# The order of a TensorE queue in one kernel: values of an attention unit ahead of the logits over cached keys

## Chip, cores, metric

One core of a Trainium2 chip (trn2) runs the whole program in one launch. The metric is the device time of an execution in microseconds. Times below are of single executions, their median, or of the one execution that the hardware profiler recorded.

## What is computed

One inference step of a two-layer decoder trunk, for a prompt group (1 x 1024 tokens) and a sample group (8 sequences x 8 new tokens, each with 1024 cached keys and values in pages). Layer 0 has stick-breaking attention beside a linear recurrence, layer 1 a chunked mixing layer; each is followed by a convolutional FFN. The part in question is the attention of layer 0, for the prompt (8 heads of 64, blocks of 128 queries) and for the samples over their caches:

```python
def sb_attend(q, k, v, bias, q_pos, k_pos):
    z = einsum('bqhd,bkhd->bhqk', q, k) * (HD_A ** -0.5) + bias
    causal = k_pos[None, :] < q_pos[:, None]
    log_keep = where(causal, log_sigmoid(-z), 0.0)
    log_after = cumsum(log_keep, axis=3, reverse=True) - log_keep
    w = where(causal, exp(log_sigmoid(z) + log_after), 0.0)
    return einsum('bhqk,bkhd->bqhd', w, v)

def sb_cached(q, k, v, bias, k_past, v_past):   # the samples: past = 1024 keys in pages, 8 new ones
    return sb_attend(q, concat([k_past, k]), concat([v_past, v]), bias, past + arange(8), arange(past + 8))
```

The kernel works with products of the probabilities 1 - sigmoid(z) instead of sums of logarithms: a scan multiplies them from the right, and the result times sigmoid(z) is the weight.

## The kernel before

**Phases.** `phase_even` does the attention, the recurrence and the projections of layer 0; a barrier of all engines follows; then `phase_rest` does the output projection of layer 0 and everything after it. The change lies in `phase_even` alone.

**Units.** `attention_units` cuts the prompt's attention into 48 units: 4 pairs of heads, for each 8 blocks of 128 queries, with at most 512 keys a unit, so that the last four blocks are two units each. A unit has n = 128 to 512 keys. For unit u:

- *logits* (TensorE, line 950, and 957 for the mask) writes two banks of PSUM, one per head;
- ScalarE takes two sigmoids from each (line 1172, `keep` and `take`);
- VectorE scans `keep` (line 1384); GpSimd multiplies `take` by it (1350, 1352);
- *weights* (TensorE, line 969) transposes n/128 tiles a head, into two banks "T";
- the copies out of these into `weights_transposed` follow: head 0 on ScalarE (line 1180), head 1 on VectorE (line 1393, `transposed`);
- *values* (TensorE, line 988, function `values`) multiplies them with `v_tokens_pair0` or `v_tokens_pair1`: 2 x n/128 matmuls, one query block's sum, which VectorE copies out (line 1403).

**Slots.** The order of work is written out by hand. `slot_order` gives the keys of a slot, and every engine walks through the same list and picks out its own. A slot has the logits of unit u and the transposes of unit u - 1; the values of unit u - 1 come behind all keys of the slot. Steps -1 to 2 lay projections between these. Step 3 has 13 slots, 0 to 12, where u runs from 36 to 48 (slot 12 has no logits, and the values of the last unit, 47). There the attention over the cached keys lies between the units, from `cached_items`. A third of it, three slots, belongs to one pair of samples s = 2p, 2p + 1:

- slots 1, 4, 7, 10 ("first slots"): L L K K K K | T T | K K K K, then W W W of the pair before (not in slot 1), then Z of the even sample;
- slots 2, 5, 8, 11: L L, V of the pair before (in slot 2: N), K K K | T T | K;
- slots 3, 6, 9, 12 ("third slots"): L L K K K K | T T | Z of the odd sample, F of the pair before (in slot 12 F stands ahead of Z; in slot 3 there is none), then the sigmoids of the pair.

Here L are a unit's logits and T its transposes. K (line 1008) transposes a cached key page's 128 columns for 512 keys, into a bank that ScalarE (line 1212) or VectorE (line 1517) empties into `ktr`, the buffer of transposed keys, of which there is one. Z (line 1022, `cached_logits`) is 8 matmuls of 512 columns over `ktr`, which add up in banks 3 and 4. W (1046, 1050) transposes the cached weights, V (1065, 1069; `last_values`, 1083 and 1087, for the last pair) multiplies them with the cached values, F (1097) gathers a pair's output. After Z of the odd sample the pair's sigmoids run on ScalarE (lines 1237 and 1239; for the last pair 1231 and 1233 in halves), then VectorE scans and multiplies (1522 and 1526; 1537 and 1542). N and P are small and run once each.

In the program's names `x_residual` holds, in this phase, `keep`, `ktr` and other buffers, `take_then_weights` holds `take`, `squares_then_scale` the samples' queries, and `v_tokens_pair` or `xb_padded` the pair's sigmoids.

**Waits.** Each engine does its queue in order. `values(u)` waits until both copies of T of unit u are done, and, where the unit opens a new sum, until the sum before it has been copied out. `cached_logits(s)` waits until the last two K of the sample (parts 6 and 7) have been copied. Semaphore `qk_done` tells the end of Z, `pv_done` that of values.

Of the kernel before, what the change touches and what calls it, by code (L numbers as in the profile page):

```python
# [547 lines left out]
def slots_of(step):  # L548
    return range(len(SIDE) + (step == 3))


def slot_order(step, slot, units):

    per = len(units) // 4
    u = per * step + slot
    first = [("L", u, 0), ("L", u, 1)] if 0 <= u < len(units) else []
    turned = [("T", u - 1, 0), ("T", u - 1, 1)] if u > 0 else []
    opened = [("O", u - 1, 0)] if u > 0 and units[u - 1][5] else []
    items = [(kind, which, group) for s, kind, which, group in side_items(step) if s == slot]
    if step < 3 or slot == 0:  # L560
        return first + turned + items + opened
    items = cached_items(slot)
    return first + items[0:4] + turned + items[4:] + opened
# [61 lines left out]
def phase_even(core, mix, k_sample, spill):  # L625
# [6 lines left out]
    with ExitStack() as ctx:  # L632
# [96 lines left out]
        def wait_emptied(eng, key):  # L729
            for who, count in banks.emptied[key]:  # L730
                eng.wait_ge(emptied_by[who], count)
# [144 lines left out]
        def in_order(step, slot):  # L876
            return slot_order(step, slot, units)

        @block.tensor
        def _(pe):  # L880
            def free(key):
                if banks.before[key]:
                    wait_emptied(pe, banks.before[key])

            def project(key, middle=None):
                kind, c, group = key
                n = slab_number(kind, group)
                a, b = CUT_USED[c]
                free(key)
                if c == 0:  # L890
                    w.wait_ready(pe, n)
                mm = None
                for k in range(KT):
                    if k == 6 and middle:
                        middle()
                    col = slice(k * P, (k + 1) * P)
                    for s, (wt, xt) in enumerate(((w.hi, act_hi), (w.lo, act_hi), (w.hi, act_lo))):
                        mm = pe.matmul(bank(key, 0, b - a), wt[:, n % 2, col], xt[:, k, a:b], start=k == 0 and s == 0,
                                       stop=k == KT - 1 and s == 2)
                mm.then_inc(filled, 1)  # L900
# [41 lines left out]
            def logits(u):  # L942
                pair, qb, lo, n, diagonal, _, _ = units[u]
                if u % PER == 0:
                    pe.wait_ge(normed, 2 * pair + 2)
                for h in range(2):
                    b = h * HD
                    key = ("L", u, h)
                    free(key)
                    mm = pe.matmul(bank(key, 0, n), mix[b:b + HD, pair, qb * P:(qb + 1) * P],  # L950
                                   kt[pair % 2][b:b + HD, lo:lo + n], start=True, stop=not diagonal,
                                   skip_group_check=True)
                    if not diagonal:
                        mm.then_inc(filled, 1)
                if diagonal:
                    for h in range(2):
                        pe.matmul(bank(("L", u, h), n - P, n), core.ident16[:, :], core.unseen[:, :], start=False,
                                  stop=True, skip_group_check=True).then_inc(filled, 1)

            def weights(u):  # L960
                n = units[u][3]
                for h in range(2):
                    key = ("T", u, h)
                    free(key)
                    pe.wait_ge(weighted, 2 * u + h + 1)
                    if not units[u][4]:
                        pe.wait_ge(edged, banks.edges[u] - 1 + h)
                    for q in range(n // P):
                        mm = pe.transpose(bank(key, q * P, (q + 1) * P), take[u % 2][h][:, q * P:(q + 1) * P],
                                          core.ident[:, :])  # L970
                    mm.then_inc(filled, 1)
# [3 lines left out]
            def values(u):  # L975
                pair, qb, lo, n, _, opens, closes = units[u]
                if u % PER == 0:
                    wait_emptied(pe, ("vt", 2, pair))
                if opens:
                    opened[pair, qb] = ("O", u, 0)  # L980
                    free(("O", u, 0))
                o = banks.bank[opened[pair, qb]]
                wait_emptied(pe, ("T", u, 0))
                wait_emptied(pe, ("T", u, 1))
                for q in range(n // P):
                    for h in range(2):
                        b = h * HD
                        mm = pe.matmul(core.ps[b:b + HD, o, 0:P], vtok[pair % 2][:, lo // P + q, b:b + HD],
                                       wtr[:, h, q * P:(q + 1) * P], start=opens and q == 0,
                                       stop=closes and q == n // P - 1, skip_group_check=True)  # L990
                mm.then_inc(pv_done, 1)

            def states():
                free(("P", 0, 0))
                pe.wait_ge(h_ready, 4)
                for j in range(4):
                    mm = pe.transpose(bank(("P", 0, 0), j * P, (j + 1) * P, 36), pk[:, j, :], core.ident[:, :])
                mm.then_inc(pk_tr, 1)
# [12 lines left out]
            def cached_logits(s):  # L1011
                u, a = s // 2, s % 2
                wait_emptied(pe, ("K", s, 6))
                wait_emptied(pe, ("K", s, 7))
                pe.wait_ge(qd_ready, 5)
                for h in range(2) if s < NSEQ - 1 else (1, 0):
                    if a == 0:
                        free(("Z", u, h))
                    if s == NSEQ - 1 and h == 0:
                        mm.then_inc(z_last, 1)  # L1020
                    for c in range(4):
                        mm = pe.matmul(core.ps[32 * c:32 * c + 32, 3 + h, :], qd[:, c, s, :],
                                       ktr[:, c, h * 512:(h + 1) * 512], start=a == 0, stop=a == 1,
                                       skip_group_check=True)
                mm.then_inc(qk_done, 1)
# [77 lines left out]
            for step in range(-1, 4):  # L1103
                for slot in slots_of(step):
                    u = PER * step + slot
                    pending = u > 0 and step < 3
                    for key in in_order(step, slot):
                        kind, which, part = key
                        if kind == "L" and part == 0:
                            logits(which)  # L1110
                        elif kind == "T" and part == 0 and step == 3:
                            weights(which)
                        elif kind in SLABS:
                            if (kind, part) == ("x", 0):
                                continue
                            project(key, (lambda: weights(u - 1)) if pending else None)
                            pending = False
                            if key == ("q", 1, 0):
                                norm.sums_pe(pe)
                        elif kind in ("r", "i"):  # L1120
                            gate(key)
                        elif kind in ("qs", "ks"):
                            square_sums(key)
                        elif kind in ("vt", "kt"):
                            rows(key)
                        elif kind == "P":
                            states()
                        elif kind == "N":
                            new_logits()
                        elif kind == "K":  # L1130
                            cached_keys(which, part)
                        elif kind == "Z":
                            cached_logits(which)
                        elif kind == "W":
                            cached_weights(which, part)
                        elif kind == "V":
                            cached_values(which)
                        elif kind == "F":
                            cached_finish(which)
                    if u > 0:  # L1140
                        values(u - 1)
            for part in (2, 1, 0):
                cached_weights(3, part)
# [1800 lines left out]
```

## Time and profile before

| | us |
|---|---|
| median of 3 runs | 2646.26 |
| the 3 runs | 2646.66, 2644.01, 2646.26 |
| the profiled execution, its own time | 2647.26 |
| its span in the trace | 2645.5 |

| engine | busy us | share of the span |
|---|---|---|
| TensorE, matmul (PE) | 2593.1 | 98% |
| VectorE (DVE) | 1608.0 | 61% |
| GpSimd (POOL) | 1132.3 | 43% |
| ScalarE (ACT) | 867.7 | 33% |

Times in rows count from the start of the span. An idle time in brackets stands ahead of a row, with what ended it. Step 3 runs from about 412 to 544 us, and is followed by the barrier. A row of matmuls counts each fp32 matmul twice: it is done in two passes.

### The profile page before, as it was taken

Reading aid. Unit: us, or ns where it says so; the run is one execution under the profiler, and the core shown is the slowest. Engines: PE = TensorE matmul, PEld = TensorE weight load, DVE = VectorE, ACT = ScalarE, POOL = GpSimd, SP = SyncE. Lnnn points to the kernel's source line nnn. Section 1 sums busy time; section 2 is a strip of 40 time slices with the busy share of each in tenths; the row PEclk is TensorE's granted clock in tenths of the full one; section 3 lists DMA queues with packets and bytes.
Section 4 is the critical chain, followed back from the end, with each engine's and each line's share of the span. In section 5 each row is a group of like instructions: output and inputs, shape, how many; then the busy total and the mean of one; then the engine's idle time right before and its main releaser. Section 6 shows DMA issues by size and latency. Waiting matters only on the chain.

```text
span 2645.5 us, 42776 instructions
## 1 busy us (share of the span) xinstructions
PE 2593.1 (98%) x16013; PEld 2423.5 (92%) x16013; DVE 1608.0 (61%) x2183; ACT 867.7 (33%) x1229; POOL 1132.3 (43%) x919
## 2 busy tenths in 40 slices
PE   8999998899999999999999999999999999999999
PEld 7878885689999999999999999999999999999998
DVE  6456566632666666666766544524766677766674
ACT  5575665533222222222222534423222222222221
POOL 3234333224544544445554411344554555544541
PEclk9999999999999999999999999999999999999999
DMA  5101107831111111111111211211111111111112
GB/s 178 57 25 44 43 25 236 274 133 41 56 49 48 48 48 48 41 47 48 48 48 33 57 40 37 60 45 56 56 41 48 48 48 48 48 40 47 48 32 71
DMA packets 208446, 164.11 MB, mean 62 GB/s; under 512 B 9902, under 2 KB 182039, under 8 KB 208335
## 3 DMA queue, kind: packets, MB, share of 16 engines
q1 hardware_dynamic: 207278, 160.35, 19.6%
q8 instruction: 79, 1.29, 0.2%
q10 hardware_dynamic: 576, 2.10, 0.2%
q14 instruction: 33, 0.26, 0.0%
q0 software_dynamic: 480, 0.11, 0.0%
HBM read 147.83 MB, written 14.69 MB: 61 GB/s over the span
## 4 chain that ended last, share of the span: by engine, by line
PE 78%; DVE 0%; ACT 0%; issue 0%; DVEq 0%
PE psum_all L148 50%; PE psum_all L2002 16%; PE psum_all L2476 6%; PE psum_all L2016 2%; PE psum_all L1990 1%; PE psum_all L1992 1%; PE psum_all L2528 0%; PE psum_all L2492 0%; PE psum_all L2516 0%; PE psum_all L2346 0%; PE psum_all L2562 0%; PE psum_all L1670 0%; DVE mixed_odd L2687 0%; ACT operand_hi_a L1775 0%; PE psum_all L2533 0%
## 5 line engine op out<-in xcount | busy, mean ns | idle before, releaser
L108 POOL TENSOR_TENSOR w_lo_part<-w_raw,w_hi_part 128x1024 fp32r<-128x1024 f32 x94 | 227.5, 2421 | 577.7 <-ACT w_hi_part L104 577.7
L2234 DVE TENSOR_TENSOR x_residual<-x_residual,psum_all 128x512 f32<-128x512 f32 (+1 forms) x616 | 449.9, 761 | 19.4
L148 PE MATMUL psum_all<-operand_hi_c,w_hi_part 128*128 128x364 f32 (+1 forms) x1344 | 297.6, 330 | 0.6 <-DVE operand_lo_c L1779 0.6
L148 PE MATMUL psum_all<-operand_hi_a,w_hi_part 128*128 128x364 f32 (+1 forms) x1344 | 297.9, 330 | 0.2 <-DVE operand_lo_a L1779 0.2
L148 PE MATMUL psum_all<-operand_hi_c,w_lo_part 128*128 128x364 f32 (+1 forms) x1344 | 295.6, 328 | 0.0
L148 PE MATMUL psum_all<-operand_lo_a,w_hi_part 128*128 128x364 f32 (+1 forms) x1344 | 295.4, 328 | 0.0
L148 PE MATMUL psum_all<-operand_hi_a,w_lo_part 128*128 128x364 f32 (+1 forms) x1344 | 295.2, 328 | 0.0
L148 PE MATMUL psum_all<-operand_lo_c,w_hi_part 128*128 128x364 f32 (+1 forms) x1344 | 295.0, 328 | 0.0
L113 POOL TENSOR_TENSOR w_lo_part<-w_raw,w_hi_part 128x1024 fp32r<-128x1024 f32 x54 | 130.6, 2419 | 373.6 <-ACT w_hi_part L97 373.6
L2218 DVE TENSOR_TENSOR gate_conv_ffn<-psum_all,gate_conv_ffn 128x1092 f32<-128x1092 f32 x48 | 62.2, 1296 | 347.3 <-PE psum_all L148 347.3
L2002 PE MATMUL psum_all<-hidden_hi_ffn,w_down_hi_ffn 128*128 128x512 f32 x616 | 240.9, 391 | 0.0
L2002 PE MATMUL psum_all<-hidden_hi_ffn,w_down_lo_ffn 128*128 128x512 f32 x616 | 240.7, 391 | 0.0
L2002 PE MATMUL psum_all<-hidden_lo_ffn,w_down_hi_ffn 128*128 128x512 f32 x616 | 239.9, 389 | 0.0
L148 PEld LDWEIGHTS psum_all<-operand_hi_a,w_hi_part 128*128 128x128 f32 x1344 | 233.5, 188 | 4.2 <-DVE operand_lo_a L1779 0.5
L148 PEld LDWEIGHTS psum_all<-operand_hi_c,w_hi_part 128*128 128x128 f32 x1344 | 233.1, 188 | 4.4 <-issue 0.8
L148 PEld LDWEIGHTS psum_all<-operand_hi_c,w_lo_part 128*128 128x128 f32 x1344 | 233.5, 188 | 0.0
L148 PEld LDWEIGHTS psum_all<-operand_hi_a,w_lo_part 128*128 128x128 f32 x1344 | 233.3, 188 | 0.0
L148 PEld LDWEIGHTS psum_all<-operand_lo_a,w_hi_part 128*128 128x128 f32 x1344 | 232.2, 188 | 0.0
L148 PEld LDWEIGHTS psum_all<-operand_lo_c,w_hi_part 128*128 128x128 f32 x1344 | 232.2, 188 | 0.0
L104 ACT ACTIVATE w_hi_part<-w_raw 128x1024 fp32r<-128x1024 f32 x94 | 99.7, 1062 | 401.1 <-PE psum_all L148 401.1
L1914 POOL TENSOR_TENSOR gate_conv_ffn<-gate_conv_ffn,rms_scale 128x1092 f32<-128x1092 f32 x48 | 122.4, 2549 | 187.8 <-ACT gate_conv_ffn L2103 187.8
L1352 POOL TENSOR_TENSOR take_then_weights<-take_then_weights,x_residual 128x511 f32<-128x511 f32 (+3 forms) x96 | 94.8, 998 | 163.6 <-DVE x_residual L1384 124.7
(354 smaller groups left out, 5042.3 us busy)
## 6 DMA issues: line engine op xcount, KB each, us to landing
w_raw<-in_w_gate_dram SPq DMA_DIRECT2D x48, 512.0 KB, 3.8
w_raw<-in_w_up_dram SPq DMA_DIRECT2D x48, 512.0 KB, 3.8
w_down_raw_ffn<-in_w_down_dram SPq DMA_DIRECT2D x44, 512.0 KB, 4.2
k_pages<-in_cache_k_dram SPq DMA_DIRECT2D x64, 256.0 KB, 3.7
v_pages<-in_cache_v_dram SPq DMA_DIRECT2D x64, 256.0 KB, 5.5
w_raw<-in_w_in_even_dram SPq DMA_DIRECT2D x20, 512.0 KB, 4.0
w_raw<-in_w_in_odd_dram SPq DMA_DIRECT2D x16, 512.0 KB, 4.8
x_spill<-x_residual SPq DMA_DIRECT2D x8, 546.0 KB, 5.3
```

Source lines behind the costliest of these rows:

```text
L104: act.activation(dst, self.raw[:, raw, :], ACT.Copy).then_inc(self.s_hi, 1)
L108: pool.tensor_tensor(lo, self.raw[:, raw, :], hi.bitcast(F32), ALU.subtract).then_inc(self.s_lo, 1)
L113: pool.tensor_tensor(dst if dst is not None else self.lo[:, par, :], self.raw[:, par, :], (hi if hi is not None else self.hi[:, par, :]).b ...
L148: mm = pe.matmul(bank[:, c, 0:width(c)], w, x[:, chunk(c)], start=(k == 0 and step == 0), stop=(k == last and step == 2))
L1352: pool.tensor_tensor(t[:, 0:n - 1], t[:, 0:n - 1], k[:, 1:n], ALU.mult).then_inc(weighted, 1)
L1914: pool.tensor_tensor(gc, gc, self.core.rb[:, :], ALU.mult).then_inc(self.gr_ready, 1)
L1990: pe.matmul(rows, b.h_smp[:, k, :], self.blocks(b.d_hi, p, 0)[:, cols], start=start and p % 2 == 0 and k == 0, stop=False, skip_group_chec ...
L2002: mm = pe.matmul(core.ps[:, base + bank, :], wt, xt[:, x, :], start=first and step == 0, stop=step == 2, skip_group_check=True)
L2016: mm = pe.matmul(bank[:, c, 0:width(c)], wt, x[:, chunk(c)], start=(k == 0 and step == 0), stop=(k == 1 and step == 2))
L2218: dve.tensor_tensor(gc, bank[:, :, 0:CH], gc, ALU.mult).then_inc(self.evac, 1)
L2234: dve.tensor_tensor(dst, dst, src, op).then_inc(self.pair_read, 1)
L2476: mm = pe.matmul(self.core.ps[:, self.lane_bank(f), 0:width(c)], wm[:, is_u, col], xm[:, k, chunk(c)], start=k == 0 and s == 0, stop=k == ...
```

## The change

In the slots that have a Z, the values of unit u - 1 are put in front of Z. In all other slots they stay at the end. There are eight Z, in the first slots 1, 4, 7, 10 and the third slots 3, 6, 9, 12. Only the TensorE queue is changed: the lists of ScalarE, VectorE, GpSimd and the DMA queue are what they were.

```diff
                     pending = u > 0 and step < 3
+                    summed = u == 0
                     for key in in_order(step, slot):
...
                         elif kind == "Z":
+                            if not summed:
+                                values(u - 1)
+                                summed = True
                             cached_logits(which)
...
-                    if u > 0:
+                    if not summed and u > 0:
                         values(u - 1)
```

TensorE's queue in slot 1, the first one with a Z: `v_tokens_pair` (L988) are the values, `x_residual,squares_then_scale` (L1022) is Z.

```order
 L1008 MATMUL psum_all<-identity,k_pages 128x128 x16
+L988 MATMUL psum_all<-weights_transposed,v_tokens_pair 64x128 x2
 L1022 MATMUL psum_all<-x_residual,squares_then_scale 32x512 x8
-L988 MATMUL psum_all<-weights_transposed,v_tokens_pair 64x128 x2
 L950 MATMUL psum_all<-x_residual,mixed_even 128x384 x2
```

The two matmuls of the values stand between the last K and Z now. T (L969) lies ahead of those 16 K.

The same engine in slot 3, where T is the last thing ahead of Z:

```order
 L1008 MATMUL psum_all<-identity,k_pages 128x128 x16
 L969 MATMUL psum_all<-identity,take_then_weights 128x128 x6
+L988 MATMUL psum_all<-weights_transposed,v_tokens_pair 64x128 x6
 L1022 MATMUL psum_all<-x_residual,squares_then_scale 32x512 x8
-L988 MATMUL psum_all<-weights_transposed,v_tokens_pair 64x128 x6
 L950 MATMUL psum_all<-x_residual,mixed_even 128x128 x2
```

The values stand right behind the transposes whose copies they read, and Z behind both.

The same engine in slot 12, the last, where the transposes of the cached weights (L1046, L1050) follow:

```order
 L969 MATMUL psum_all<-identity,take_then_weights 128x128 x8
 L1097 MATMUL psum_all<-query_selector,own_outputs 128x32 x2
+L988 MATMUL psum_all<-weights_transposed,v_tokens_pair 64x128 x8
 L1022 MATMUL psum_all<-x_residual,squares_then_scale 32x512 x8
-L988 MATMUL psum_all<-weights_transposed,v_tokens_pair 64x128 x8
 L1046 MATMUL psum_all<-identity,v_tokens_pair 8x128
```

The values stood between Z and W here; now Z and W are neighbours.

## Rows read from the trace of the kernel before

**Rows 1.** Windows: busy time by engine, step 3 and all after it.
```profile
core 0: us, PE busy (x) PEld busy (x) DVE busy (x) ACT busy (x) POOL busy (x), PEclk, DMA share, GB/s
412.00:545.00 133.00, 109.67 (x1372) 77.49 (x1372) 73.39 (x101) 64.65 (x124) 26.32 (x31) 0.95 0.77 258
545.00:2645.50 2100.50, 2092.27 (x12080) 2009.76 (x12080) 1289.93 (x1721) 549.42 (x721) 953.39 (x733) 1.00 0.16 50
```

**Rows 2.** Timeline, slot 1: start us, us, engine, line, operation [idle before <-releaser].
```profile
422.92 0.28 DVE L1393 COPY weights_transposed<-psum_all 128x128 f32<-128x128 f32 x1
...
425.54 0.69 DVE L1517 COPY x_residual<-psum_all 128x512 f32<-128x512 f32 x1 [0.41 <-PE psum_all L1008]
...
426.33 1.92 PE L1022 MATMUL psum_all<-x_residual,squares_then_scale 128*32 128x512 f32 x16 [0.83 <-ACT x_residual L1212]
...
428.19 0.44 PE L988 MATMUL psum_all<-weights_transposed,v_tokens_pair 128*64 128x128 f32 x4
```

**Rows 3.** Timeline, slot 4: Z of the third sample.
```profile
451.60 1.92 PE L1022 MATMUL psum_all<-x_residual,squares_then_scale 128*32 128x512 f32 x16
```

**Rows 4.** Timeline, slots 3 and 4: Z, values, and the way back to TensorE.
```profile
440.19 0.54 DVE L1393 COPY weights_transposed<-psum_all 128x384 f32<-128x384 f32 x1
...
440.37 1.92 PE L1022 MATMUL psum_all<-x_residual,squares_then_scale 128*32 128x512 f32 x16 [1.03 <-ACT weights_transposed L1180]
...
442.22 0.88 PE L988 MATMUL psum_all<-weights_transposed,v_tokens_pair 128*64 128x128 f32 x12
442.35 1.11 ACT L1237 ACTIVATE xb_padded<-psum_all,row_bias 128x1024 f32<-128x1024 f32 x1 [2.44 <-PE psum_all L1022]
...
443.49 2.31 DVE L1522 TENSOR_TENSOR_SCAN xb_padded<-xb_padded,all_ones 128x1032 f32<-128x1032 f32 x1 [2.76 <-ACT xb_padded L1237]
...
448.24 0.66 PE L969 MATMUL psum_all<-identity,take_then_weights 128*128 128x128 f32 x4 [1.53 <-DVE x_residual L1517]
```

**Rows 5.** Timeline, slots 6 and 7.
```profile
466.99 1.93 PE L1022 MATMUL psum_all<-x_residual,squares_then_scale 128*32 128x512 f32 x16
467.07 0.69 DVE L1393 COPY weights_transposed<-psum_all 128x512 f32<-128x512 f32 x1 [0.18 <-PE psum_all L969]
...
469.84 1.09 PE L988 MATMUL psum_all<-weights_transposed,v_tokens_pair 128*64 128x128 f32 x16
...
478.12 1.53 PE L1008 MATMUL psum_all<-identity,k_pages 128*128 128x128 f32 x12 [1.52 <-DVE x_residual L1517]
```

**Rows 6.** Timeline, slots 9 and 10.
```profile
499.00 0.54 DVE L1393 COPY weights_transposed<-psum_all 128x384 f32<-128x384 f32 x1
499.17 1.93 PE L1022 MATMUL psum_all<-x_residual,squares_then_scale 128*32 128x512 f32 x16 [1.24 <-issue]
...
501.59 0.88 PE L988 MATMUL psum_all<-weights_transposed,v_tokens_pair 128*64 128x128 f32 x12
...
509.89 1.53 PE L1008 MATMUL psum_all<-identity,k_pages 128*128 128x128 f32 x12 [1.15 <-DVE x_residual L1517]
```

**Rows 7.** Timeline, slot 12 and what follows it.
```profile
527.93 0.69 DVE L1393 COPY weights_transposed<-psum_all 128x512 f32<-128x512 f32 x1 [0.18 <-PE psum_all L969]
...
528.19 1.92 PE L1022 MATMUL psum_all<-x_residual,squares_then_scale 128*32 128x512 f32 x16
...
530.04 1.09 PE L988 MATMUL psum_all<-weights_transposed,v_tokens_pair 128*64 128x128 f32 x16
...
532.16 0.27 PE L1046 MATMUL psum_all<-identity,v_tokens_pair 128*8 128x128 f32 x1 [1.03 <-DVE v_tokens_pair L1542]
...
534.08 1.09 PE L1050 MATMUL psum_all<-identity,v_tokens_pair 128*128 128x128 f32 x4 [1.17 <-DVE v_tokens_pair L1542]
```

**Rows 8.** Windows around the end of the step; the granted clock is in column PEclk.
```profile
530.00:534.00 4.00, 1.89 (x25) 1.36 (x21) 3.89 (x5) 2.58 (x6) 0.00 (x0) 1.00 0.67 249
534.00:540.80 6.80, 6.72 (x104) 4.97 (x108) 0.14 (x1) 0.58 (x1) 0.00 (x0) 0.50 0.02 5
```

**Rows 9.** Timeline, cached values at the one clock and at the other.
```profile
455.53 1.96 PE L1065 MATMUL psum_all<-v_pages,x_residual 128*32 128x128 f32 x64
...
535.68 1.94 PE L1087 MATMUL psum_all<-v_pages,x_residual 128*32 128x128 f32 x32
```

## Prediction, made before the changed kernel had run

> **What bounds the kernel now.** I read the windows first [rows 1]. Behind the barrier, from 545 us on, TensorE is busy 2092.27 of 2100.50 us; whatever the change shifts in front of the barrier, that part follows by the same amount, since its first work waits for the barrier and nothing in it has room to catch up. So the question is by how much step 3 ends earlier or later. In step 3 TensorE is busy 109.67 of 133.00 us, 23 us idle; VectorE has 73.39 and ScalarE 64.65. No engine is full, so the step is bound by TensorE's queue together with the handovers to and from ScalarE and VectorE. Next I read the timeline slot by slot, at the eight Z: did TensorE wait ahead of Z, for what, when had the copies been done that the values read, and who waits for the end of Z?
>
> **What the change removes, adds and moves.** No instruction is added or removed. Eight groups of values move ahead of Z. Each edit has two effects: values fill a wait ahead of Z, if their own inputs have come by then; and Z ends later by the length of the values plus any wait for their inputs. Successive groups overlap by some 0.07 us (the Z row is 1.92 us long and the next row starts 1.86 later [rows 2]), so the values of slot 1 cost 0.37 us where their row shows 0.44, and by the same step 0.81 and 1.02 where rows show 0.88 and 1.09. An engine's end reaches TensorE some 0.1 us later: in slot 1 VectorE's copy of the last K ends at 425.54 + 0.69 = 426.23, and Z starts at 426.33 [rows 2]. I take 0.09.
>
> *First slots (1, 4, 7, 10).* The four K behind T give the copies of T time to end. In slot 1 the copy was done at 423.20, and TensorE stood idle 0.83 us ahead of Z, for the copies of the last K [rows 2]. The values, 0.37 us, fit into that. Z starts as before, and the next logits start 0.37 us earlier: **-0.37 us**. In slot 4, W lies between the K and Z, and Z starts with no wait [rows 3]; slots 7 and 10 read the same. There Z is exchanged with values at no gap: the next logits start when they did, and Z's later end (1.02 us in slot 4) is waited for by nobody soon, because these are even samples, whose sum goes on with the odd sample two slots later; the next copies into `ktr` come only behind V and a unit's logits. **0 us** for three slots. If that cover were gone, each would cost the length of its values, up to 1.02.
>
> *Third slots (3, 6, 9, 12).* Here T is the last thing ahead of Z. The change puts the values right behind the T whose copy they wait for; that copy is at the end of VectorE's queue. Before, Z covered it. Queued behind the waiting values is Z, and for Z wait ScalarE's sigmoids, for these VectorE's scan.
>
> - Slot 3: the copy ends at 440.19 + 0.54 = 440.73 [rows 4]. Values start at 440.82, Z at 441.63 where it started at 440.37: +1.26. The row puts Z's idle time down to a copy of line 1180; by the times it is VectorE's last K copy, which the copy of T follows.
> - Slot 6: the copy ends at 467.76. Values at 467.85, Z at 468.87 instead of 466.99 [rows 5]: +1.88. There was no wait ahead of Z here.
> - Slot 9: the copy ends at 499.54. Values at 499.63, Z at 500.44 instead of 499.17 [rows 6]: +1.27.
> - Slot 12: the copy ends at 528.62. Values at 528.71, Z at 529.73 instead of 528.19 [rows 7]: +1.54.
>
> Does all of it count? The next logits are later by the wait alone (Z and values changed places): 1.26 - 0.81 = 0.45, 0.86, 0.46 us. But the path that ends last goes another way. In slot 3: Z ends, ScalarE's sigmoid of 1.11 us starts 0.06 later, VectorE had waited 2.76 us for it and starts its scan, and behind scan, multiply and the next unit's scan stands the K copy for which TensorE waits 1.53 us in slot 4 [rows 4]. That wait is real idle time, so this chain decides, and it hangs on Z's end. The same pattern stands in slots 7 and 10, with waits of 1.52 and 1.15 us for the same copy [rows 5, 6]. In slot 12 the chain is shorter: Z, sigmoids by halves, scan, multiply, W, where TensorE waits 1.03 and 1.17 us [rows 7]; all of the delay counts, and the values that used to fill part of that hole are gone from it. So I count Z's delay in full: 1.26 + 1.88 + 1.27 + 1.54 = **+5.95 us**. The low bound is the delay of the logits in the first three and the chain in the last: 0.45 + 0.86 + 0.46 + 1.54 = 3.31.
>
> A gain elsewhere in those slots: values end earlier, so VectorE can copy the query block out (line 1403) earlier. That copy stands behind scan and multiply in VectorE's queue and finds its input ready in both orders: 0.
>
> Sum: 5.95 - 0.37 = **+5.58 us**. Against the profiled execution that is 2647.26 + 5.58 = 2652.8; that execution lies 1.0 above the median, so against the median 2651.8.
>
> A rule on queues is to be weighed here, since it decides whether a waiting group holds Z up. The row shows the K copy and then Z in queue order [rows 2], and no row shows a matmul that waits while a later one starts. The Trainium skill ("PSUM — Partial Sum Buffer", section "Engine vs sequencer instructions") says that matmuls start and complete in program order. By it Z can't pass the waiting values and the 5.95 stand; could it pass them, they would be 0. The trace of before can't tell, having no such wait ahead of Z.
>
> **The clock.** After two waits of 1.03 and 1.17 us with little between, TensorE was granted 0.50 (1.2 GHz) from 534.0 to 540.8 us instead of 1.00 (2.4 GHz) [rows 7, 8]. In that stretch 32 passes of a shape take 1.94 us where 64 took 1.96 at full clock [rows 9]: half of 6.8, some 3.4 us, is lost. After the change the hole ahead of W is wider: Z ends, and 2.1 us pass (1.03 + 1.02 + the overlap). So I expect a fall there again, a little earlier, so that part of it lies over waits; I take no change, between -1 and 0.
>
> **Rivals.**
>
> 1. *The clock falls once more.* Slot 6 gets a wait of 0.9 us ahead of the values, and in slots 4, 7 and 10 the waits behind the logits grow by up to 1.0 (Z's delay less the logits') beside those of 1.53, 1.52 and 1.15. For it: after slot 12 two such waits were enough. Against: before, none of these three was. It costs half of what is executed meanwhile, up to 3.4 and about 2.5 since some is waiting: 2651.8 + 2.5 = 2654.3, slower. The Trainium skill ("TensorE: Matmul & The Clock Gate", "What's actually happening") says that the gate goes by how busy TensorE has been recently; [rows 8] agree, and by that rule more idle time in a slot makes this rival likelier.
> 2. *The clock doesn't fall in slot 12.* The fall came after 2.2 us of waits in about 3; with another alignment it may stay away. Then 2651.8 - 3.4 = 2648.4, no difference. That one of three runs took 2644.01, 2.3 below the median, fits executions without it.
> 3. *The chain has slack that I overlook*, and only the logits' delay carries: 3.31 - 0.37 = 2.94, so 2649.2, no difference.
> 4. *Faster.* The waits ahead of Z (0.83, 1.03, 1.24 us [rows 2, 4, 6]) are what the change fills, and the copy of T reaches TensorE before that of the last K. Then values hide in slots 1, 3 and 9, 0.37 + 0.81 + 0.81 = 2.0 us, and Z isn't delayed. For a result outside the bound the clock must also stay up at the end, 3.4 more: 2646.26 - 5.4 = 2640.9. It decides at the order of the two copies on VectorE; in slots 3 and 9 the copy of T ends last, at 440.73 and 499.54, after Z had started. That speaks strongly against it.
>
> **How the numbers follow.** A measurement of this kernel can tell some 0.2% from no change, 5.3 us, here 2651.6. My forecast, 2651.8 (0.45), lies right on that line and is split: 0.25 slower, 0.20 same. Rival 1: 0.24, slower. Rival 2: 0.12, same. Rival 3: 0.13, same. Rival 4: 0.06, faster. So slower 0.49, same 0.45, faster 0.06. The range leaves out rival 4 and the far tail of rival 1: 2648.0 to 2655.5.
>
> **What the profile after would show.** In slots 3, 6, 9 and 12: a wait ahead of line 988 for line 1393 of about 1.5, 0.9, 1.7 and 0.5 us (from where TensorE's wait for Z began, 440.37 - 1.03 in slot 3, to the start of values), no wait ahead of 1022; in slot 1 values straight behind K and then the rest, 0.46, of the old 0.83. TensorE's wait for line 1517 in slots 4, 7 and 10 still there, and step 3 5.6 us longer. Step 3 longer by only 3 means rival 3; a row of windows at 0.50 before 520 us means rival 1; none after 530 means rival 2. The sum would be wrong if VectorE did its copies at another time than before: then Z's delay isn't the sum of wait and values.

## The result, and the profile after

| | before | after |
|---|---|---|
| median of 7 runs, us | 2646.62 | 2655.97 |
| lowest and highest | 2644.01, 2649.05 | 2651.08, 2657.02 |
| profiled execution, its own time | 2647.26 | 2655.99 |
| its span | 2645.5 | 2654.3 |

The ratio is 1.0027 with a 95% interval of 1.0018 to 1.0036: the change makes the kernel slower, by 4.8 to 9.5 us. The median lies 0.5 us above my range. The medians differ by 9.4 us and the means by 7.4, since the changed kernel's seven times lie in two groups (three from 2651.1 to 2652.2, four from 2656.0 to 2657.0) and its median belongs to the upper one.

Line numbers of the changed kernel are 4 higher behind the edit (1397 is 1393, 1241 is 1237, and so on). In rows, a transpose (lines 969, 1008, 1046, 1050) counts once and only the other fp32 matmuls twice: in slot 3 the queue has six of line 969 and six of line 988, and the rows have x6 and x12. First the timeline of slots 3 and 4, which answers to [rows 4]; columns are start us, us, engine, line, operation, and the idle time ahead with what ended it:

```profile
438.59 0.54 DVE L1397 COPY weights_transposed<-psum_all 128x384 f32<-128x384 f32 x1
439.27 1.34 PE L988 MATMUL psum_all<-weights_transposed,v_tokens_pair 128*64 128x128 f32 x12 [1.54 <-DVE weights_transposed L1397]
440.54 3.09 PE L1022 MATMUL psum_all<-x_residual,squares_then_scale 128*32 128x512 f32 x16
...
443.71 1.11 ACT L1241 ACTIVATE xb_padded<-psum_all,row_bias 128x1024 f32<-128x1024 f32 x1 [5.40 <-PE psum_all L1022]
...
444.86 2.31 DVE L1526 TENSOR_TENSOR_SCAN xb_padded<-xb_padded,all_ones 128x1032 f32<-128x1032 f32 x1 [5.73 <-ACT xb_padded L1241]
...
446.49 1.15 PE L1008 MATMUL psum_all<-identity,k_pages 128*128 128x128 f32 x8 [1.34 <-ACT take_then_weights L1176]
...
449.60 0.65 PE L969 MATMUL psum_all<-identity,take_then_weights 128*128 128x128 f32 x4 [1.52 <-DVE x_residual L1521]
```

Values wait 1.54 us for VectorE's copy of T, as forecast, Z stands behind them, then sigmoid and scan follow as before, and in slot 4 TensorE waits for the K copy as long as before: 1.52 us against 1.53. Z's own inputs were there earlier (VectorE's last K copy ended at 438.66), yet Z started only behind the waiting values. One thing was not forecast: Z takes 3.09 us instead of 1.92. The clock fell here.

That the wait for the K copy is no longer than before doesn't mean that slot 4 lost nothing. TensorE already waits longer at an earlier handover, 1.34 us at 446.49 where it was 0.51 before:

```profile
445.12 1.15 PE L1008 MATMUL psum_all<-identity,k_pages 128*128 128x128 f32 x8 [0.51 <-ACT take_then_weights L1172]
```

The K copy then comes later by the same amount: TensorE goes on 6.03 us after the slot's logits (449.60 less 443.57), against 5.21 before (448.24 less 443.03). In slots 7 and 10 the extra idle time stands ahead of the first transposes that wait for a K copy (0.88 and 0.85 us, before 0.20 and 0.21).

The same wait in slots 6, 9 and 12 (0.87, 1.75 and 0.51 us), and what follows in slots 7, 10 and 12, from TensorE's timeline [rows 5 to 7]:

```profile
469.27 1.09 PE L988 MATMUL psum_all<-weights_transposed,v_tokens_pair 128*64 128x128 f32 x16 [0.87 <-DVE weights_transposed L1397]
...
481.43 1.53 PE L1008 MATMUL psum_all<-identity,k_pages 128*128 128x128 f32 x12 [1.52 <-DVE x_residual L1521]
...
502.98 0.88 PE L988 MATMUL psum_all<-weights_transposed,v_tokens_pair 128*64 128x128 f32 x12 [1.75 <-DVE weights_transposed L1397]
...
514.52 2.76 PE L1008 MATMUL psum_all<-identity,k_pages 128*128 128x128 f32 x12 [1.16 <-DVE x_residual L1521]
...
535.05 1.09 PE L988 MATMUL psum_all<-weights_transposed,v_tokens_pair 128*64 128x128 f32 x16 [0.51 <-DVE weights_transposed L1397]
...
540.05 0.27 PE L1046 MATMUL psum_all<-identity,v_tokens_pair 128*8 128x128 f32 x1 [2.05 <-DVE v_tokens_pair L1546]
```

And slot 1, where the values go into the wait ahead of Z, of which 0.46 us are left [rows 2]:

```profile
424.20 0.44 PE L988 MATMUL psum_all<-weights_transposed,v_tokens_pair 128*64 128x128 f32 x4
425.10 1.92 PE L1022 MATMUL psum_all<-x_residual,squares_then_scale 128*32 128x512 f32 x16 [0.46 <-issue]
```

**Where the time went.** From TensorE's timelines I took the start of each slot's logits (line 950) and the distance from one to the next; slots not named differ by at most 0.01 us.

| stretch | before | after | more | forecast |
|---|---|---|---|---|
| slot 1 to 2 | 15.62 | 14.17 | -1.45 | -0.37 |
| 3 to 4 | 8.95 | 11.09 | 2.14 | 0.45 |
| 4 to 5 | 11.44 | 12.26 | 0.82 | 0.81 |
| 6 to 7 | 8.03 | 8.94 | 0.91 | 0.86 |
| 7 to 8 | 12.14 | 13.17 | 1.03 | 1.02 |
| 9 to 10 | 9.54 | 10.06 | 0.52 | 0.46 |
| 10 to 11 | 12.82 | 15.31 | 2.49 | 0.81 |
| 11 to Z of 12 | 12.98 | 14.57 | 1.59 | 1.54 |
| that Z to the last line 1097 | 14.59 | 13.07 | -1.52 | 0 |
| sum | | | 6.52 | 5.58 |

(The forecast gave Z's delay; split over a pair of slots it is the logits' delay and the rest.) Four stretches differ from the forecast by over 0.1 us, and in all four the granted clock changed. In the windows of the profile after, PEclk (third value from the end) is 0.50 in five short stretches up to 556 us; four of these, a half microsecond of each, and the windows around a sixth:

```profile
441.00:441.50 0.50, 0.50 (x8) 0.10 (x4) 0.00 (x0) 0.00 (x0) 0.00 (x0) 0.50 1.06 410
...
515.00:515.50 0.50, 0.50 (x4) 0.50 (x3) 0.06 (x1) 0.00 (x0) 0.05 (x1) 0.50 0.00 0
...
542.50:543.00 0.50, 0.50 (x5) 0.17 (x3) 0.00 (x0) 0.00 (x0) 0.00 (x0) 0.50 0.00 0
...
552.50:553.00 0.50, 0.50 (x5) 0.50 (x4) 0.42 (x1) 0.50 (x2) 0.00 (x0) 0.50 0.28 82
...
1490.00:1494.00 4.00, 4.00 (x22) 2.39 (x20) 2.88 (x2) 2.49 (x3) 2.50 (x1) 1.00 0.01 2
1494.00:1498.00 4.00, 4.00 (x15) 4.00 (x16) 0.47 (x1) 3.18 (x5) 3.45 (x2) 0.57 0.00 0
```

Each lasts 3.4 us. Before there were two of 6.8 us, behind 534 us [rows 8] and in slot 1, of which this window is a part:

```profile
420.00:424.00 4.00, 4.00 (x21) 4.00 (x20) 2.18 (x4) 1.26 (x3) 0.64 (x1) 0.50 1.05 381
```

So slot 1 and the end of the step got shorter, slots 3 and 10 longer. Behind line 1097 the kernel loses another 2.4 us (8.8 of span less 6.4), where the clock is at 0.50 behind the barrier and again behind 1494 us. These two falls can't be put down to the new order: in the kernel with the change in the first slots alone, whose time is that of before, the clock fell behind the barrier too, and no other kernel's profile has the one at 1494 us.

### The profile page after: what moved, and what is told of

Same layout as the page of the kernel before. It is cut to its first block, busy times and chain, and to the rows that moved or that the text cites. A ratio compares the mean times of both kernels' runs of the same rounds, so it can differ in the third digit from the quotient of the medians.

```text
span 2654.3 us, 42776 instructions
## 1 busy us (share of the span) xinstructions
PE 2596.3 (98%) x16013; PEld 2425.2 (91%) x16013; DVE 1606.5 (61%) x2183; ACT 867.4 (33%) x1229; POOL 1133.4 (43%) x919
## 4 chain that ended last, share of the span: by engine, by line
PE 78%; DVE 0%; ACT 0%; issue 0%; DVEq 0%
PE psum_all L148 50%; PE psum_all L2006 16%; PE psum_all L2480 6%; PE psum_all L2020 2%; PE psum_all L1994 1%; PE psum_all L1996 1%; PE psum_all L2496 1%; PE psum_all L2532 0%; PE psum_all L2520 0%; PE psum_all L2350 0%; PE psum_all L2566 0%; PE psum_all L1674 0%; DVE mixed_odd L2691 0%; ACT operand_hi_a L1779 0%; PE psum_all L194 0%; PE psum_all L2537 0%
```

## Experiments

Each kernel was timed in 5 rounds beside the kernel before; each says which of the two it edits.

**Each half of the change alone.** Values ahead in the third slots only, on the changed kernel:

```diff
-                            if not summed:
+                            if not summed and which % 2:
```

> Values ahead of Z in the third slots 3, 6, 9, 12 only; the first slots as before. My theory (Z is held up by the copy of T, and its end decides by way of ScalarE and VectorE): Z is late by 1.26, 1.88, 1.27 and 1.54 us, step 3 ends 5.9 us later than before at equal clock, some 2652 us. Rival (the end of Z has slack, only the next logits count): 3.3 us later, 2650 us. Rival (the order costs little and the loss is the clock's): the shift from slot to slot at full clock is under 1 us.

Measured: 2654.9 us against 2646.85, ratio 1.0030 (1.0018 to 1.0042), 2.9 us above the expected 2652. The Z are late by 1.98, 1.95, 1.32 and 1.59 us, in slot 3 with a fall of the clock, which the expectation left out. TensorE's waits ahead of the values:

```profile
439.86 1.54 PE L988 MATMUL psum_all<-weights_transposed,v_tokens_pair 128*64 128x128 f32 x12 [1.53 <-DVE weights_transposed L1397]
...
469.86 1.09 PE L988 MATMUL psum_all<-weights_transposed,v_tokens_pair 128*64 128x128 f32 x16 [0.88 <-DVE weights_transposed L1397]
...
503.57 0.88 PE L988 MATMUL psum_all<-weights_transposed,v_tokens_pair 128*64 128x128 f32 x12 [1.74 <-DVE weights_transposed L1397]
...
535.57 1.09 PE L988 MATMUL psum_all<-weights_transposed,v_tokens_pair 128*64 128x128 f32 x16 [0.51 <-DVE weights_transposed L1397]
```

They are those of the full change to 0.01 us. The loss sits in these four slots, as far as these intervals can tell. The reverse condition, `which % 2 == 0`, keeps the first slots alone:

> Values ahead of Z in the first slots 1, 4, 7, 10 only; the third slots as before. My theory: 0.37 us gained in slot 1, where values fill part of the wait of 0.83 us ahead of Z, and nothing in slots 4, 7, 10: 2646.2 us, not to be told from before; in the trace the logits of slot 2 are 0.4 us earlier. Rival (Z's later end costs there as well): up to 1 us lost in each of slots 4, 7 and 10, 2649 us.

Measured: 2647.22 us against 2646.85, ratio 1.0001 (0.9992 to 1.0010), no difference. In slot 1:

```profile
425.34 0.44 PE L988 MATMUL psum_all<-weights_transposed,v_tokens_pair 128*64 128x128 f32 x4
426.24 1.92 PE L1022 MATMUL psum_all<-x_residual,squares_then_scale 128*32 128x512 f32 x16 [0.46 <-issue]
428.09 0.92 PE L950 MATMUL psum_all<-x_residual,mixed_even 64*128 64x384 f32 x4
```

From Z to the next logits it is 1.85 us; before it was 2.23 (28.56 less 26.33). That is a gain of 0.38 us, forecast 0.37, too little for the measured time to show. Slots 3 to 11 take their old time to 0.01 us, so Z's later end costs nothing in slots 4, 7 and 10. The rival there falls.

**Does the place of T make the wait?** On the changed kernel, on all engines, the two T of a third slot between the second and third K:

```diff
-    return first + items[0:4] + turned + items[4:] + opened
+    at = 2 if slot % 3 == 0 else 4
+    return first + items[0:at] + turned + items[at:] + opened
```

> The changed kernel with the two T of the third slots put between the second and the third K, on all engines, so that two K lie between T and the values that wait for its copies. If the position of T is what makes the values wait, TensorE's waits of 1.54, 0.87, 1.75 and 0.51 us ahead of line 988 vanish, and Z waits for the last K copy instead: late against before by 0.5 to 1.1 us in each third slot and no longer by 1.3 to 1.9, step 3 some 3 us shorter than in the changed kernel: 2651 to 2653 us. If the wait is for something else, 2655 us.

Measured: 2652.46 us, ratio to before 1.0021 (1.0011 to 1.0031). The waits in slots 3 and 9, in slot 3 with VectorE's scan and copy ahead:

```profile
436.80 1.75 DVE L1389 TENSOR_TENSOR_SCAN x_residual<-x_residual,all_ones 128x512 f32<-128x512 f32 x1
...
438.47 0.53 DVE L1398 COPY weights_transposed<-psum_all 128x384 f32<-128x384 f32 x1
...
439.14 0.88 PE L989 MATMUL psum_all<-weights_transposed,v_tokens_pair 128*64 128x128 f32 x12 [0.75 <-DVE weights_transposed L1398]
...
499.73 0.88 PE L989 MATMUL psum_all<-weights_transposed,v_tokens_pair 128*64 128x128 f32 x12 [0.96 <-DVE weights_transposed L1398]
```

I expected them to vanish. They only halve, since VectorE reaches the copy of T behind its own scan of the second head. In slots 6 and 12 they are gone. Z is late by 0.72, 1.05, 0.72 and 1.02 us, within the expected 0.5 to 1.1, but not by a wait for the last K copy, as I had expected: it starts right behind the values. Together that is 3.5 us in place of the 6.15 of the table below. So the position of T sets the price, by the place of its copy in VectorE's queue.

This kernel also tells whether Z's end decides. The logits of slots 4, 7 and 10 come as early as before (-0.09, +0.02, -0.08 us), and still each of these slots takes longer up to the next logits, by 0.82, 1.03 and 0.81 us. The two together are 0.73, 1.05 and 0.73, which is Z's delay, in a step where the clock fell only ahead of slot 2 and at the end. If only the logits' delay counted, these sums would be near 0.

**Can the wait be made longer on purpose?** Here VectorE's scan of the second head stands behind the second K copy, one place later than before:

```diff
-                        if apart and key == order[3]:
+                        if apart and key == order[5]:
                             scan(order[1][1], 1)
```

Two kernels: this edit on before, and on the changed one.

> The kernel before, with VectorE's scan of the second head moved behind the second K copy in the first and third slots of step 3 (it stood between the two). In the trace that scan takes 1.75 to 1.90 us while GpSimd multiplies, 1.23 us else, and Z or TensorE's next K waits for the copy behind it. If the path that decides goes through VectorE's queue, Z of the third slots starts up to 1 us earlier and the waits of 1.52 and 1.15 us in slots 7 and 10 go: 3 to 6 us gained, 2641 to 2644 us. If the end of Z has slack, no more than 1 us.

> The late scan on the changed kernel. The copy of T that the values of the third slots read now stands behind a scan of 1.2 us, while the last K copy, for which Z alone waits, is earlier. If the order of values and Z costs by holding Z up for that copy, the change costs more here than without the late scan: Z late against the late scan alone by some 2.4, 1.5, 2.4 and 1.5 us, 7 to 8 us in sum, 2651 us or more. If the cost of the change is anything that does not hang on this copy, it stays at 6 us or becomes less, 2650 us or below.

Measured: late scan alone 2643.70 us, ratio to before 0.9988 (0.9979 to 0.9997); with the change 2653.38, 1.0023 (1.0014 to 1.0032). The change costs 9.7 us here by the medians, against 7 to 8 expected, but it cost 9.4 without the late scan, and with these intervals the times can't tell the two costs apart. The trace can. Slot 3 without the change, where Z follows close on the K copy:

```profile
438.08 0.69 DVE L1517 COPY x_residual<-psum_all 128x512 f32<-128x512 f32 x1 [0.71 <-PE psum_all L1008]
438.69 1.21 DVE L1384 TENSOR_TENSOR_SCAN x_residual<-x_residual,all_ones 128x512 f32<-128x512 f32 x1
438.87 1.92 PE L1022 MATMUL psum_all<-x_residual,squares_then_scale 128*32 128x512 f32 x16 [0.18 <-issue]
```

And with it, slots 3, 6 and 9:

```profile
440.19 0.88 PE L988 MATMUL psum_all<-weights_transposed,v_tokens_pair 128*64 128x128 f32 x12 [1.80 <-DVE weights_transposed L1397]
...
468.81 1.09 PE L988 MATMUL psum_all<-weights_transposed,v_tokens_pair 128*64 128x128 f32 x16 [1.18 <-DVE weights_transposed L1397]
...
502.58 1.55 PE L988 MATMUL psum_all<-weights_transposed,v_tokens_pair 128*64 128x128 f32 x12 [1.86 <-DVE weights_transposed L1397]
```

Z is late by 2.43, 2.26, 3.16 and 1.60 us (part of the 3.16 at the lower clock), 9.45 us in all where the change alone has 6.15. In slot 3 the logits are late by 1.62 us and the next slot adds 0.81, together Z's 2.43. Start of Z, measured from the start of the slot's logits (slot 12: from slot 11's):

| slot | forecast | after | after, filled | T early | late scan, with less without |
|---|---|---|---|---|---|
| 3 | 1.26 | 1.77 | 1.31 | 0.72 | 2.43 |
| 6 | 1.88 | 1.94 | 1.94 | 1.05 | 2.26 |
| 9 | 1.27 | 1.33 | 1.32 | 0.72 | 3.16 |
| 12 | 1.54 | 1.59 | 1.58 | 1.02 | 1.60 |

**Does the chain behind Z decide?** The multiply behind the scan of cached logits, 1.23 us on VectorE, given to GpSimd for the first three pairs, on before and on the changed kernel:

```diff
-                dve.wait_ge(after_done, u + 1)
-                dve.wait_ge(taken_s, 2 * u + 2)
-                dve.tensor_tensor(take_s[:, 0:NEW - 1], take_s[:, 0:NEW - 1], keep_s[:, 1:NEW], ALU.mult
-                                  ).then_inc(w_ready, 1)
...
+            def cached_weighted(u):
+                pool.wait_ge(after_done, u + 1)
+                pool.wait_ge(taken_s, 2 * u + 2)
+                pool.tensor_tensor(take_s[:, 0:NEW - 1], take_s[:, 0:NEW - 1], keep_s[:, 1:NEW], ALU.mult
+                                   ).then_inc(w_ready, 1)
...
```

> The kernel before, with the multiply behind the scan of cached logits (line 1526, 1.23 us on VectorE) moved to GpSimd for the first three pairs. If TensorE's waits of 1.53, 1.52 and 1.15 us in slots 4, 7 and 10 are the end of the chain Z, sigmoid, scan, multiply, next scan, K copy, they shrink by up to 1.23 us each: step 3 ends 3 to 3.6 us earlier, 2643 us. If that chain has slack (rival), the waits stay and the time is 2646.5 us.

> The same move of the multiply to GpSimd, on the changed kernel. My theory: the chain from Z's end still decides in slots 4, 7 and 10, so the change costs here, against the kernel with the multiply moved alone, the same 5 to 6 us as without the move: some 2649 us. If 1.23 us less on the chain lets TensorE's own queue decide (only the logits' delay counts), it costs 3.3 us or less against it, 2647 us or less.

Measured: 2646.83 us, ratio 0.9999 (0.9990 to 1.0008), and with the change 2653.87, 1.0029 (1.0019 to 1.0040). The 3 us didn't come, though the chain lost 1.23 us of work three times. Slot 7 shows why:

```profile
471.94 2.01 POOL L1357 TENSOR_TENSOR v_tokens_pair<-v_tokens_pair,xb_padded 128x1031 f32<-128x1031 f32 x1 [5.52 <-DVE xb_padded L1530]
...
472.26 2.77 DVE L1392 TENSOR_TENSOR_SCAN x_residual<-x_residual,all_ones 128x512 f32<-128x512 f32 x1 [0.22 <-ACT x_residual L1172]
```

The scan takes 2.77 us where one alone takes 1.21 to 1.23. It ends 1.08 us after GpSimd's multiply (475.03, 473.95). What VectorE was spared, it waits. From the logits of slot 4, 7 and 10 to the next ones it is 11.34, 12.65 and 12.21 us, against 11.44, 12.14 and 12.82 before: -0.10, +0.51, -0.61. So this run doesn't decide as it was meant to. That the lengthening in slot 7 reaches TensorE speaks for the chain, and so does the late scan, which shortens VectorE's path without GpSimd: logits of slots 7 to 8 come in 10.99 in place of 12.14 us, 10 to 11 in 12.01 in place of 12.82 (4 to 5 stays at 11.41 against 11.44); TensorE's waits of 1.52 and 1.15 us for the K copy are gone there, with 0.38 and 0.34 left for the copy of T. These two show that VectorE's queue decides in slots 7 and 10; that Z's end does, in all three, is shown by the kernel with T early. The cost of the change with the multiply moved is 7.0 us by the medians, above the expected 5 to 6. Z is late there, against the kernel with the multiply moved alone, by 1.32, 1.95, 1.32 and 1.60 us, as without the move; part of the 7.0 is the clock, which falls for 6.8 us in slot 7 of its profile.

**How much is the clock?** On the changed kernel, transposes of no use into a free part of bank 7, in five of TensorE's waits. At each place the filling stands behind a wait for what last read bank 7; the order of all else stays:

```diff
+            def fill(count):
+                for _ in range(count):
+                    pe.transpose(core.ps[:, 7, 384:512], core.ident[:, :], core.ident[:, :])
...
                         elif kind == "Z":
+                            if not summed and which in (1, 3, 5):
...
+                                fill((6, 3, 7)[which // 2])
                             if not summed:
                                 values(u - 1)
...
+            pe.wait_ge(o_stored, 3)
+            fill(8)
             for part in (2, 1, 0):
                 cached_weights(3, part)
+                if part == 1:
+                    fill(4)
```

> The changed kernel with transposes of no use put into TensorE's own waits: 6, 3 and 7 of them ahead of the values of slots 3, 6 and 9, and 8 between Z and the last transposes of weights, 4 between the two halves of these. The order of all else is that of the changed kernel. If the loss beyond the order's own 6 us is the clock, the stretches at 0.50 in slot 3 and at the end of step 3 vanish, and the runs gather at the lower end of the changed kernel's, 2651 us or less. If the clock has no part, the time is 2656 us, or more where the filling delays a step.

Measured: 2651.57 us, ratio to before 1.0018 (1.0009 to 1.0027), 4.4 us below the changed kernel's median, and above the 2651 expected by 0.6. The intervals of the two ratios to before overlap (1.0009 to 1.0027, and 1.0018 to 1.0036), so of the 4.4 us only the direction is likely; the profile shows more. TensorE's rows of slots 3 and 12:

```profile
439.27 0.88 PE L988 MATMUL psum_all<-weights_transposed,v_tokens_pair 128*64 128x128 f32 x12 [0.88 <-DVE weights_transposed L1411]
...
540.15 0.27 PE L1046 MATMUL psum_all<-identity,v_tokens_pair 128*8 128x128 f32 x1 [1.03 <-DVE v_tokens_pair L1560]
```

The values of slot 3 take 0.88 us again, not 1.34, and the distance from the logits of slot 3 to those of slot 4 is 9.45 us: 0.50 above before, forecast 0.45. The useless work delays no values: they start at 439.27 in both kernels, and the Z of slots 6, 9 and 12 are as late as in the changed one. In slots 7 and 10, whose waits were not filled, the clock still fell (L1008 x12 took 2.27 and 2.82 us). The same filling, 4 + 4, in slot 12 of the kernel before:

> The kernel before, with 4 + 4 transposes of no use in the two waits of slot 12 (1.03 and 1.17 us). If these waits bring the clock down to 0.50 for the cached values of the last pair, the stretch behind 534 us stays at 1.00 and up to 3.4 us are gained: 2643 to 2645 us. If the clock falls for another reason, 2646.8 us.

Measured: 2645.03 us, ratio 0.9994 (0.9985 to 1.0003), not separable from before by the interval. The last group of cached values runs in

```profile
536.08 2.83 PE L1087 MATMUL psum_all<-v_pages,x_residual 128*32 128x128 f32 x96
```

where it took 4.10 us before. In its profile nothing behind slot 1 is below 1.00 until the last microseconds, and from Z of slot 12 to line 1097 it is 11.54 us in place of 14.59, 3.05 less. The median moved by 1.9 only, which would fit if not every execution of before had that fall; that is argued, not shown.

**A kernel from the parts.** Values ahead in the first slots alone, the late scan, and the filling 4 + 4 in slot 12, on the changed kernel's code:

> Three parts together: values ahead of Z in the first slots alone (0.4 us), VectorE's scan of the second head behind the second K copy (3 to 4 us of step 3), and 4 + 4 transposes of no use in the waits of slot 12 (up to 3.4 us of clock). If the parts add up, 2641 to 2642 us, below both kernels; if TensorE's wait of 1.21 us for a DMA at the end of step 3, seen with the late scan, takes back what the filling gives, as with the late scan alone, 2643.5 us.

Measured: 2639.46 us, ratio to before 0.9974 (0.9963 to 0.9985), below both kernels: 7.4 us less than before and 16.5 less than the changed one. It is less than the expected 2641 to 2642, too; the parts alone gave 3.2 (late scan), 1.9 (filling) and none (first slots), so some 2 us of the gain are not accounted for by them. In its profile the clock is at 0.50 only in slot 1. The end of slot 12:

```profile
528.18 0.27 PE L1046 MATMUL psum_all<-identity,v_tokens_pair 128*8 128x128 f32 x1 [0.44 <-DVE v_tokens_pair L1554]
...
530.10 0.63 PE L1050 MATMUL psum_all<-identity,v_tokens_pair 128*128 128x128 f32 x4 [0.73 <-DVE v_tokens_pair L1554]
...
532.46 2.83 PE L1087 MATMUL psum_all<-v_pages,x_residual 128*32 128x128 f32 x96
```

The 96 passes take 2.83 us; before they took 4.10. The wait of 1.21 us for a DMA, seen in the profile of the late scan alone, isn't in this one; whether it was chance I did not test.

## Why the prediction was right, and where it was not

- **First slots.** Right: -0.38 in slot 1 (measured 2.23 less 1.85 us in the kernel with that part alone), 0 in slots 4, 7 and 10.
- **Third slots.** Right in mechanism and size: values wait for VectorE's copy of T, Z behind them. Forecast 1.26, 1.88, 1.27, 1.54; at full clock 1.31, 1.94, 1.32, 1.58, together 6.15 against 5.95. The 0.05 more each time is the way from the end of a copy to TensorE: 0.14 us (439.13 to 439.27), where I had taken 0.09.
- **All of it counts.** Right. The logits are late by 0.50, 0.91 and 0.52, and the slot behind brings the rest, 0.82, 1.03 and 0.81 (the last from the kernel with T early, where it ran at full clock). The chain is the one forecast, though the extra idle time shows at earlier waits than the one for the K copy. Rival 3, slack, falls by the kernel with T early, where Z's delay counts in full while the logits have none.
- **The queue.** Right: Z, with its own inputs there, didn't pass the waiting values.
- **The clock stays up in slot 12 (rival 2).** It fell there, but for 3.4 us in place of 6.8.
- **Faster (rival 4).** The copy of T came last in slots 3 and 9, as the rows said. It falls, but a piece of it was real: slot 1.
- **The clock.** This is the term that was mis-sized. I took no change, between -1 and 0, for the end of the step, where it was -1.5 in this profile, and gave rival 1 one more fall and a chance of 0.24. The profile has new falls in slots 3 and 10, behind the barrier and at 1494 us, and shorter ones in slots 1 and 12. The span grew by 8.8 us, of which the order takes 5.8 (5.58 and the 0.2 above), so the clock's net share is 3.0. It fits the windows: six stretches of 3.4 us at 0.50 against two of 6.8 before are 6.8 us more at half clock, at most 3.4 us lost (an estimate). Of this the new order need not have brought the last two falls. Filling five waits took 4.4 us off the median, with intervals that overlap. The forecast and rival 1 should have been one case: the order's 5.6 and some clock on top. I had seen that waits grow in three slots and treated the fall as an exception.
- **What was luck.** The three lower times lie 4.5 to 5.5 us above the median before, no more than the order's share, and the four upper ones 9.4 to 10.4; in which group the median falls was not forecast.
- What stays open: why the changed kernel's seven runs lie in two groups (2651.1 to 2652.2, and 2656.0 to 2657.0). Their mean granted clocks, 0.998 and 0.995 to 0.996, fit the clock as the difference; what decides in a single execution they don't say.

## What to carry to other kernels

Moving work into a wait pays only if its own inputs are there first: look for the engine that makes them, and at what stands ahead of that copy in its queue. In a chain from engine to engine the item on the chain goes first, and independent work behind it, where it covers the next handover; a group ahead of it costs its length plus its wait. Waits can also cost by TensorE's clock: in slot 12 of the kernel before, two waits of 1.03 and 1.17 us stood ahead of 6.8 us at 0.50, and with these waits filled the stretch was 3.05 us shorter.

## What the runs showed of the hardware

VectorE's scan is held up by GpSimd. In the changed kernel, slot 3:

```profile
435.91 1.09 POOL L1356 TENSOR_TENSOR take_then_weights<-take_then_weights,x_residual 128x511 f32<-128x511 f32 x1 [3.77 <-DVE x_residual L1388]
...
436.33 1.75 DVE L1388 TENSOR_TENSOR_SCAN x_residual<-x_residual,all_ones 128x512 f32<-128x512 f32 x1
```

The scan ends 1.08 us after the multiply (438.08, 437.00), as it did with the longer multiply above, so it seems to stand until GpSimd is done and then to run nearly whole (1.08 of the 1.21 to 1.23 us that it takes alone); beside the same multiply a copy out of PSUM (435.75 to 436.42) took its usual 0.67 us. With the late scan it runs behind the multiply and takes 1.21 us, 0.54 less. The Trainium skill ("SBUF — State Buffer", "SBUF: two separate sides") says that a VectorE operation with two SBUF inputs and a GpSimd operation that reads SBUF exclude each other on a shared pair of ports, and that the one that starts first keeps it for its whole instruction. The two durations agree.

The clock can fall with no wait right ahead: from 1490 to 1494 us TensorE shows 4.00 of 4.00 us busy, mostly with transposes of 128x128 and 64x64, weight loads busy for 2.39, and behind that PEclk is 0.57 over the next 4 us. The other eleven kernels run the same code there, and none of their profiles has a fall in it, so the order of the work there does not decide by itself. And transposes can hold it up: with nothing but 4 + 4 of them put into the last waits, the stretch behind stayed at 1.00 in both profiles that have them (the kernel before with filling, and the kernel from the parts).
